# Expert stage: w_down read in row pairs, gate/up columns taken in matching order, and token slots dealt round the partitions

## The reference: what is computed

```
for each row: a router picks 1 of 4 groups, then 2 of the 8 experts inside it
a   = h @ w_gate[e]            # (1024 x 256), 32 experts in all
b   = h @ w_up[e]              # (1024 x 256)
y  += c * ((silu(a) * b) @ w_down[e])   # w_down[e] is (256 x 1024)
```

## Time and profile before

| what | value |
|---|---|
| median of 3 runs | 1103.2 us (1102.49 to 1106.08) |
| the profiled execution, first to last instruction (span) | 1100.9 us |
| TensorE busy in the span | 86% |
| expert stage, first gather to last scatter landed | 679 to 1044 us |

### The profile page before, as it was taken

How to read it: one execution, slowest core, us unless ns; L and a number is a source line. 1 busy time by engine, 2 the same in 40 slices (tenths; PEclk the granted TensorE clock), 3 DMA queues, 4 the chain that set the end, 5 groups by cost and what they waited for, 6 DMA issues and landing times.

```text
span 1100.9 us, 15827 instructions
## 1 busy us (share of the span) xinstructions
PE 947.3 (86%) x6165; PEld 899.3 (82%) x6165; DVE 572.0 (52%) x742; ACT 306.2 (28%) x490; POOL 241.0 (22%) x168
## 2 busy tenths in 40 slices
PE   5799789887999989999899992999999999999500
PEld 5799689787999889999688882999999999999400
DVE  6313997888879662232622436344444444444275
ACT  6321111210111552221302330233323233232243
POOL 0009970044233000000000011112222121221134
PEclk9899989897999999999899995999999999999755
DMA  8011011101111112110323427689999999994192
GB/s 258 1 58 39 19 38 40 34 29 31 55 38 48 48 30 65 58 48 29 93 89 115 172 82 291 236 335 349 329 359 329 361 339 354 356 339 182 29 368 102
DMA packets 78796, 169.93 MB, mean 154 GB/s; under 512 B 10763, under 2 KB 48155, under 8 KB 70561
## 3 DMA queue, kind: packets, MB, share of 16 engines
q1 hardware_dynamic: 69537, 152.05, 39.0%
q0 software_dynamic: 9216, 17.32, 4.7%
HBM read 156.83 MB, written 22.47 MB: 163 GB/s over the span
## 4 chain that ended last, share of the span: by engine, by line
PE 72%; issue 12%; DVE 8%; ACT 4%; DMA 2%; POOL 2%; POOLq 0%; DVEq 0%; SPq 0%; ACTq 0%
PE ps L1343 29%; PE ps L1576 21%; PE ps L1516 8%; PE ps L1560 8%; DVE x L1331 3%; PE ps L1546 2%; POOL w_lo L583 1%; PE ps L1495 1%; PE ps L1436 1%; DVE hT L1087 1%; PE ps L1353 1%; ACT sq L900 1%; PE ps L1487 1%; ACT C L791 1%; DMA yy<-YK 1%
## 5 line engine op out<-in xcount | busy, mean ns | idle before, releaser
L1343 PE MATMUL ps<-hT,w_hi 128*128 128x352 f32 x1344 | 334.9, 331 | 35.0 <-POOL w_lo L583 17.6
L1343 PEld LDWEIGHTS ps<-hT,w_hi 128*128 128x128 f32 x1344 | 241.0, 194 | 37.2 <-issue 34.1
L1576 PEld LDWEIGHTS ps<-XT,wgu 128*128 128x128 f32 x2048 | 236.6, 194 | 5.1 <-ACT XT L859 2.6
L1576 PE MATMUL ps<-XT,wgu 128*128 128x104 f32 x2048 | 236.5, 277 | 2.1 <-ACT XT L859 2.1
L1343 PE MATMUL ps<-hT,w_lo 128*128 128x352 f32 x672 | 221.5, 330 | 0.0
L1343 PEld LDWEIGHTS ps<-hT,w_lo 128*128 128x128 f32 x672 | 129.0, 192 | 0.0
L1012 DVE SCALAR_TENSOR_TENSOR C<-V,w_dw,C 128x1086 f32<-128x1086 f32 x80 | 111.1, 1458 | 0.2 <-issue 0.2
L1286 DVE TENSOR_TENSOR wdn_lo<-wdn,wdn_hi 128x1024 fp32r<-128x1024 f32 x64 | 75.6, 1222 | 53.9 <-ACT wdn_hi L881 53.9
L1516 PE MATMUL ps<-wo_hi,hT 128*128 128x512 f32 x288 | 92.6, 403 | 4.7 <-DVE hT L1087 4.5
L920 DVE TENSOR_TENSOR w_lo<-w_raw,w_hi 128x1024 fp32r<-128x1024 f32 (+1 forms) x30 | 37.8, 1259 | 105.7 <-ACT w_hi L676 105.7
L636 POOL DMA_INDIRECT YK<-Y,s_now x32 | 32.7, 1022 | 268.7 <-DVE Y L1260 268.7
(11 more groups left out here) (208 smaller groups left out, 1264.1 us busy)
## 6 DMA issues: line engine op xcount, KB each, us to landing
wgu<-in_w_gate SPq DMA_DIRECT2D x32, 1024.0 KB, 9.3
wgu<-in_w_up SPq DMA_DIRECT2D x32, 1024.0 KB, 13.8
wdn<-in_w_down SPq DMA_DIRECT2D x32, 1024.0 KB, 7.3
w_raw<-in_w_in SPq DMA_DIRECT2D x28, 512.0 KB, 3.7
yy<-YK SPq DMA_DIRECT2D x8, 1024.0 KB, 12.2
xs<-in_x_prompt SPq DMA_DIRECT2D x8, 512.0 KB, 6.8
wo_raw<-in_w_out SPq DMA_DIRECT2D x8, 512.0 KB, 3.8
xr<-in_x_prompt SPq DMA_DIRECT2D x16, 256.0 KB, 2.8
```

Of the source, the lines that this page charges most:

```text
L1343: m = pe.matmul(ps[:, bank, 0:CH], a[:, s, w + k, :], r[:, w + k, c * CH:(c + 1) * CH], start=(k == 0 and q == 0), stop=(k == K - 1 and q ...
L1576: m = pe.matmul(ps[:, 2 + b, o:o + CAP], wgu[u][:, h, c, f * P:(f + 1) * P], XT[:, b, c, 0:CAP], start=(c == 0), stop=(c == KD - 1))
```

## The change

Three edits. w_down's rows 2p and 2p + 1 go to partition p. The stationary columns of gate and up are f, f + 2, f + 4, ... (a step of two elements, 8 bytes) in place of 128 neighbours, so that the activation's rows come out in the same order as w_down's. The row of slot numbers is no longer 0 to 103 in order: place 8a + b holds a + 13b (a from 0 to 12, b from 0 to 7), so the pair of rank r goes to partition 8 (r mod 13) + r div 13.

```diff
-            down_v = I["w_down"][0].rearrange("g e (c p) d -> (g e) p c d", p=P)
+            down_v = I["w_down"][0].rearrange("g e (p c) d -> (g e) p c d", p=P)
...
-            link(pool.iota(slot_i[:], pattern=[[1, CAP]], base=0, channel_multiplier=0))
+            link(pool.iota(slot_i[:].rearrange("p (a b) -> p a b", b=8), pattern=[[1, CAP // 8], [CAP // 8, 8]], base=0, channel_multiplier=0))
...
-                            m = pe.matmul(ps[:, 2 + b, o:o + CAP], wgu[u][:, h, c, f * P:(f + 1) * P], XT[:, b, c, 0:CAP],
+                            m = pe.matmul(ps[:, 2 + b, o:o + CAP], wgu[u][:, h, c, f:F:KF], XT[:, b, c, 0:CAP],
                                           start=(c == 0), stop=(c == KD - 1))
```

## The result

The changed kernel takes 1113.5 us (median of 4 runs, 1112.9 to 1115.5) against 1103.8 us for the kernel before in the same session: a ratio of 1.0088, 95% interval 1.0072 to 1.0105. It is slower by some 9.8 us, outside the range of the prediction. The profiled execution has a span of 1111.7 us, 10.8 more than before.

The account below looks back on a forecast made before the run. TensorE was taken to bound the loop, with DMA latency on the path at its two ends. Terms 0 + 0 - 0.9 - 0.73 = -1.6 us gave 1101.6 us from 1103.2; range 1098.8 to 1104.8 us.

Parts of the forecast that it names:

- Gate and up columns with a step of two: 2048 weight loads of L1576 reading every second element; taken to cost 0 us.
- the bounds of 0 and 136 us: Limits for the stepped weight loads' cost: nothing, or DVE's factor of 1.6 for steps applied to each load.
- The rival: L1576's weight loads feel the step: up to 136 us slower, so up to 1238 us; chance 0.12.
- a tenth of that is 1115: Total time in us if the stepped L1576 loads cost a tenth of the 136 us.
- The sign of being wrong: In L1576, 64 products taking more than 7.4 us would show the prediction wrong.
- w_down in row pairs, worth nothing: w_down loads in 8 KB instead of 4 KB pieces: 0 us, since transfers have slack behind TensorE.
- The slots, -1.6 us: Occupied rows spread over more DMA engines: first gather 0.9 us shorter, last scatter 0.73 us shorter.
- The rival of no gain: Gather and scatter gain nothing: rows not dealt in blocks of 8, or memory sets their pace; 1103.2 us, chance 0.15.
- The blocks of 8: Gather and scatter: 104 partitions cut in 13 blocks of 8 neighbours, one DMA engine to a block.
- the rival of turns of four: Partitions go to eight engines in turns of four; fullest keeps 8 rows, no gain; within a rival of chance 0.15.
- The clock, either way: TensorE's low clock at the loop's ends: gives back 2.7 us (chance 0.15) or takes as much (0.08).

Follow-up runs that it names:

- e9: Kernel before with only 36 of the 104 columns of XT moved in the gate and up products, columns contiguous: 1296.8 us.
- e10: Kernel before with only 36 of the 104 columns of XT moved and the step of two columns in the gate and up products: 1250.5 us.
- e1: Kernel before with the new slot numbers alone: median 1102.8 us, ratio 0.9985 to before.
- e2: Kernel after with contiguous gate and up columns again, keeping new slots and w_down in row pairs: median 1102.6 us, ratio 0.9983 to before.
- e6: Kernel before, but from the fifth expert on only an eighth of gate and up is loaded, columns contiguous: 1104.0 us.
- e3: Kernel before with the step of two gate and up columns alone: median 1117.7 us, ratio 1.0117 to before.
- e4: Kernel before with gate and up columns at a step of 4 elements, taken across the row blocks: 1369.4 us.
- e5: Kernel before with gate and up columns at a step of 8 elements, taken across the row blocks: 1411.2 us.
- e8: Kernel before with gate and up columns at a step of 3 elements, taken across the row blocks: 1226.8 us.

## Why the prediction was wrong

**The step that failed** is "Gate and up columns with a step of two": "A step of 8 bytes is far nearer to the plain 4 than to DVE's 32 and more, so I take 0". The term is +6 ns x 2048 = +12.5 us. Much of its working stands. The load sets the pace of the stream, there is no room below it, and a slower load shows 2048 times; e9 and e10 confirm it. What was wrong is the choice between the bounds of 0 and 136 us by nearness. The load's time is not a slope in the step but the larger of two times, and steps of 2, 3 and 4 cost +0.006, +0.06 and +0.12 us. No row spoke for 0 rather than for a few per cent, and with 2048 loads behind each ns, 5% of a load is four times what the measurement can resolve. The rival stood there with a chance of 0.12. Its upper end of 136 us was eleven times too high; "a tenth of that is 1115" came within 2 us, but the tenth was taken from no row, so that is luck. The sign of being wrong, 64 products in more than 7.4 us, is what the profile shows (7.51).

Two readings behind this step were off. The upper bound came from L1137, taken as a row with steps of 8 elements on its inputs. In the kernel these inputs are split as `r (p c) -> r p c`, with c last: they are read in order. Only the output is stepped, by 128 elements. So the earlier trace rows has no stepped read at all, and neither bound came from one. And the 0.115 us is 7.34 / 64, where 7.34 us runs from the first load's start to the last one's end, one load's own length included; the distance in the chain of the earlier trace rows is 7.12 / 64 = 0.111 us.

The Trainium skill's line rule (SBUF — State Buffer, "Door 1: The DMA port swizzle") says that two hits on a 16-byte line are enough for full speed. The runs are close to it and not with it: two hits to a line cost 5%, 0.1173 us in place of 0.1113.

**w_down in row pairs, worth nothing:** right, e1 and e2 agree. The reason given, slack of the transfers behind TensorE, fits e6 as well: halving the traffic changed nothing.

**The slots, -1.6 us:** right in kind, the parts off in both directions. The scatter gave 0.41 us in place of 0.73. The view of queue 0 over the last scatter's packets, 1053.3 to 1054.9 us of the kernel after, to be read with the earlier trace rows:

```profile
q0 software_dynamic: 144, 0.25, 56.1%
```

That is 9.0 of 16 engines on average over 1.6 us, where 7.2 worked over 1.95 and 11 to 12 were forecast for 1.2. The work per row stayed (9.0 x 1.6 / 60 = 0.24 us); it is spread wider, but does not end evenly. The rival of no gain is settled: the last scatter takes 3.42 or 3.43 us in the three profiles with the new slots and 3.83 to 3.85 in the nine with the old. The blocks of 8 are in keeping with this but not shown; no run dealt the rows another way. (In the rival of turns of four, the rows would not have crowded on the same eight engines, as the prediction has it, but on every second one; the fullest would still have had 8 rows, so its price stands.) The gather gave 0.66 us between the two profiles and 1.1 us by the means of all (5.07 in nine, 3.99 in three), where 0.9 was forecast.

**The clock, either way:** it gave back 1.1 us on average on the first expert's products in the three profiles with the new slots (9.33 in place of 10.47). This was a rival, with 2.7 us. The other end showed no such gain: the last down product takes 4.81 us before and 4.83 after, but 5.47 in e1 and e2, 5.38 in e3 and 4.36 to 5.47 over all profiles, without a pattern that follows the edits.

**The sum with what is now known:** +12.5 - 1.1 - 0.4 - 1.1 = +9.9 us; measured +9.8. So close a match is partly luck: the same three gains make -2.6 us for e1, where the medians give -1.8, with 0.7 us lost again in the last down product of its profile. What stays open is small: e3 less the kernel after is 0.29% of the time, while e1 less the kernel before is 0.15%; the intervals do not exclude that these are the same.

## What to carry to other kernels

Where a stream is bound by its weight loads, look for another place for a reordering before putting a step into the stationary operand (in the DMA's pattern, say, which was not tried here): a step of two float32 cost 5% of each load, three 55%, four 110%. Larger transfers were worth nothing here, because the compute engine never waited for one. The rows tell it beforehand: the loads land 7 to 14 us after issue and are used over 30 us later. The indirect DMAs at the two ends of the loop, whose rows fill only part of the partitions, gained from spreading them; those in the middle of the loop are hidden beneath TensorE.

## What was not expected

- The price of a stepped weight load follows the lines touched (1.79 to 1.83 ns each at steps of 2, 3 and 4), above a floor of 0.111 us.
- At the low clock level a step of two is free (0.216 us either way), and at a step of four the clock level makes little difference (14.79 to 15.23 us a stream).
- Moving fewer columns under the same loads made the kernel 17% slower (1296.8 against 1104.0 us), since the granted clock fell to 0.61 in a loop in which TensorE was busy throughout. Of the two, the kernel with the slower loads was the faster (1250.5 us, clock 0.71). Why it kept more of the clock was not tried.
- The clock also left its high level in e4 and e5, in whose loop TensorE has no idle time but each load takes 0.23 or 0.24 us (0.70 to 0.80 on average in e4's loop, 0.67 in e5's), and stayed there in e8 (1.00 between 740 and 1000 us).
